# Strassen's seven products for the gate and up projections of a decoder block on one Trainium2 core

## What is computed

```python
h2 = rmsnorm(x, norm2_w[layer]) * (1.0 + sc2) + sh2
ffn = (jax.nn.silu(h2 @ w_ffn_gate[layer]) * (h2 @ w_ffn_up[layer])) @ w_ffn_down[layer]
x = x + g2 * ffn
return rmsnorm(x, final_norm_w)
```

## Time and profile before

| | |
|---|---|
| time, 3 runs | 1796.13 to 1798.64 us, median 1796.4 |
| the profiled execution's own time | 1798.21 us |
| its span, first to last instruction | 1796.4 us |
| TensorE matmul busy | 1673.2 us, 93% |
| VectorE busy | 851.3 us, 47% |
| ScalarE busy | 619.6 us, 34% |
| GpSimd busy | 282.8 us, 16% |
| mean granted TensorE clock | 0.968 |
| DMA over the span | 154.76 MB, mean 86 GB/s |

### The profile page before, as it was taken

One profiled execution on the slowest core, in us unless ns is written; L12 is line 12 of the kernel. 1 busy time (PEld: TensorE's weight loads), 2 busy tenths in 40 slices (PEclk: granted clock), 3 DMA queues, 4 the chain that ended last, 5 costly groups with the idle time before them and its releaser, 6 DMA issues.

```text
span 1796.4 us, 21138 instructions
## 1 busy us (share of the span) xinstructions
PE 1673.2 (93%) x8115; PEld 1355.4 (75%) x8115; DVE 851.3 (47%) x1412; ACT 619.6 (34%) x941; POOL 282.8 (16%) x215
## 2 busy tenths in 40 slices
PE   4997999999999989999999789999999999999996
PEld 2783477888888868877877568888888887887875
DVE  4677999654856667554434631111111111234333
ACT  5326412355665665562123321111111111232232
POOL 1311022244443522230002200000000000002002
PEclk8998999999999999999999889999999999999998
DMA  9561211321212150003443301111111111422231
GB/s 330 186 231 42 71 48 47 100 77 47 65 47 71 59 182 1 1 1 129 153 164 123 111 24 47 52 53 47 47 47 47 47 49 56 188 93 82 101 128 52
DMA packets 124293, 154.76 MB, mean 86 GB/s; under 512 B 8382, under 2 KB 90425, under 8 KB 124220
## 3 DMA queue, kind: packets, MB, share of 16 engines
q1 hardware_dynamic: 115578, 134.91, 22.8%
q10 hardware_dynamic: 8066, 16.78, 2.5%
q0 software_dynamic: 576, 2.10, 0.3%
HBM read 132.25 MB, written 20.99 MB: 85 GB/s over the span
## 4 chain that ended last, share of the span: by engine, by line
PE 73%; issue 14%; DVE 6%; ACT 3%; POOL 2%; DMA 1%; SPq 0%; POOLq 0%; DVEq 0%; ACTq 0%
PE pp L502 20%; PE pp L504 19%; PE pp L503 19%; PE pp L1258 5%; PE pp L1264 3%; PE pp L1443 3%; PE pp L1552 2%; DVE arena L1808 2%; DVE h_tmp L2129 1%; POOL x L822 1%; PE pp L1281 1%; DVE h_raw L1778 0%; ACT arena L975 0%; POOL x1b L827 0%; DVE h_lo L2135 0%
## 5 line engine op out<-in xcount | busy, mean ns | idle before, releaser
L497 DVE TENSOR_TENSOR w_lo<-raw,w_hi 128x1024 fp32r<-128x1024 f32 x112 | 142.5, 1273 | 441.8 <-ACT w_hi L492 441.8
L492 ACT ACTIVATE w_hi<-raw 128x1024 fp32r<-128x1024 f32 x112 | 118.6, 1059 | 523.9 <-PE pp L504 523.9
L502 PE MATMUL pp<-h_hi,w_hi 128*128 128x512 f32 x704 | 276.0, 392 | 13.6 <-DVE h_lo L2135 13.6
L503 PE MATMUL pp<-h_lo,w_hi 128*128 128x512 f32 x704 | 275.6, 391 | 0.0
L504 PE MATMUL pp<-h_hi,w_lo 128*128 128x512 f32 x704 | 275.5, 391 | 0.0
L502 PE MATMUL pp<-hT_hi,e_hi 128*128 128x512 f32 x416 | 168.2, 404 | 7.4 <-POOL hT_lo L721 6.0
L1830 DVE TENSOR_SCALAR_CACHE_REDUCE arena<-arena,bound 128x384 bf16<-128x384 f32 (+2 forms) x192 | 169.4, 941 | 0.8
L502 PEld LDWEIGHTS pp<-h_hi,w_hi 128*128 128x128 f32 x704 | 133.3, 189 | 41.8 <-DVE h_lo L2135 14.1
L504 PE MATMUL pp<-hT_hi,e_lo 128*128 128x512 f32 x416 | 164.3, 395 | 0.0
L503 PE MATMUL pp<-hT_lo,e_hi 128*128 128x512 f32 x416 | 164.2, 395 | 0.0
L503 PEld LDWEIGHTS pp<-h_lo,w_hi 128*128 128x128 f32 x704 | 133.3, 189 | 27.8
(11 more groups left out here) (229 smaller groups left out, 2816.8 us busy)
## 6 DMA issues: line engine op xcount, KB each, us to landing
arena<-in_w_ada SPq DMA_DIRECT2D x48, 512.0 KB, 8.0
raw<-in_w_ffn_down SPq DMA_DIRECT2D x44, 512.0 KB, 3.2
arena<-in_w_in SPq DMA_DIRECT2D x33, 512.0 KB, 3.6
raw<-in_w_ffn_gate SPq DMA_DIRECT2D x22, 512.0 KB, 3.6
raw<-in_w_ffn_up SPq DMA_DIRECT2D x22, 512.0 KB, 3.7
gates_t<-arena ACTq DMA_DIRECT2D x32, 256.0 KB, 2.1
gate_in<-gates_t SPq DMA_DIRECT2D x8, 1024.0 KB, 5.3
raw<-in_w_out SPq DMA_DIRECT2D x16, 512.0 KB, 3.2
```

What stands on the lines that cost most here:

```text
L492: act.activation(w_hi[n % 2][:, :], raw[:, n % 4, :], ACT.Copy).then_inc(hi_ready, 1)
L497: dve.tensor_tensor(w_lo[n % 2][:, :], raw[:, n % 4, :], w_hi[n % 2][:, :].bitcast(F32), ALU.subtract).then_inc(lo_ready, 1)
L502: nc.tensor.matmul(out, ah, bh, start=start and k == 0, stop=False)
L503: nc.tensor.matmul(out, ah, bl, start=False, stop=False)
```

## The change

Two hidden tiles form a pair (11 pairs). For each pair and each matrix (m = 0 gate, m = 1 up) the product is a 2x2 block product: two hidden tiles by two feature halves, times two feature halves by two token halves. Strassen's scheme does it in seven block products instead of eight. A block product is four k slices of 128x128 by 128x512, 12 matmuls. The order of the 14 products of a pair is in `FIRST` and `LATER`; every engine's queue is written as steps n, in which it first does what follows from product n-4 and then prepares the weights of product n.

- The sums of weight blocks are new: GpSimd (`weight_sum`) for five of seven products, then ScalarE (hi) and VectorE (lo), 512 wide, in a ring of four buffers.
- The sums of h2 blocks (`cb_sum`) are made once, during the first pair, by GpSimd and VectorE; all seven combinations are kept as hi and lo.
- The results of products 2, 5 and 1 are copied out of their banks by ScalarE, mixed by GpSimd (`mix_parts`), and VectorE adds the other products' banks (`combine`, six steps for each matrix and pair).
- ScalarE's Silu and VectorE's product with it (`gate_hidden`) follow once for each of four blocks. The hidden values go to memory (`hid_d`, two stores of 512 KB for each pair, issued by SP) and come back for the down steps, 256 KB a step, in the same queue as the weights.
- The hardware loop now has four passes over two pairs (28 products); three pairs stand ahead of it.

The diff, cut to its core (GpSimd's and ScalarE's side of the h2 combinations, buffer addresses and the renaming of one helper are left out):

```diff
-    h2_hi, h2_lo = rounded("h2_hi", 24576, KD, SEQ), rounded("h2_lo", 32768, KD, SEQ)
-    xn2 = [x1[:, t, :] for t in range(4)] + [own(f"xn2_{t}", B0 + D * t, D) for t in range(4)]
-    h2_tmp = [own(f"h2_tmp{i}", D0 + HALF * i, HALF) for i in range(2)]
-    hidT = own("hidT", A0, KF * SEQ)
+    COMBO = {2: 24576, 4: 28672, 1: 0, 3: 4096, 5: 8192, 7: 12288, 6: 16384}
+    cb_hi = {q: rounded(f"cb_hi{q}", o, 4, HALF) for q, o in COMBO.items()}
+    cb_lo = {q: rounded(f"cb_lo{q}", o + 2048, 4, HALF) for q, o in COMBO.items()}
+    cb_sum = {q: own(f"cb_sum{q}", o + 2048, 4, HALF) for q, o in COMBO.items()}
+    h2_part = [[own(f"h2_part{f}{t}", 32768 + 2048 * (f + 2 * t), 4, HALF) for t in range(2)] for f in range(2)]
+    xn2 = [x1[:, t, :] for t in range(4)] + [own(f"xn2_{t}", B0 + D * t, D) for t in range(4, NT)]
+    wp_at = [22528, 23552, 40960, 41984]
+    wp_hi = [rounded(f"wp_hi{i}", o, HALF) for i, o in enumerate(wp_at)]
+    wp_lo = [rounded(f"wp_lo{i}", o + HALF, HALF) for i, o in enumerate(wp_at)]
+    wp_sum = [own(f"wp_sum{i}", o + HALF, HALF) for i, o in enumerate(wp_at)]
+    stage = [own(f"stage{j}", 36864 + SEQ * j, SEQ) for j in range(2)]
+    hid_in = [own(f"hid_in{i}", 34816 + HALF * i, HALF) for i in range(4)]
...
+    FF_PAIRS = KF // 2
+    FIRST = [(m, q) for q in (2, 4, 5, 1, 3, 7, 6) for m in range(2)]
+    LATER = [(m, q) for m in range(2) for q in (2, 5, 1, 4, 3, 7, 6)]
+    PER = len(FIRST)
+    S_DN = S_FF + PER * FF_PAIRS
+    PEELED, TURNS = 3, (FF_PAIRS - 3) // 2
+    WEIGHTS_OF = {1: ((0, 0), (1, 1), ALU.add), 2: ((1, 0), (1, 1), ALU.add), 3: ((0, 0),), 4: ((1, 1),), 5: ((0, 0), (0, 1), ALU.add),
+                  6: ((1, 0), (0, 0), ALU.subtract), 7: ((0, 1), (1, 1), ALU.subtract)}
+    INPUTS_OF = {1: ((0, 0), (1, 1), ALU.add), 2: ((0, 0),), 3: ((0, 1), (1, 1), ALU.subtract), 4: ((1, 0), (0, 0), ALU.subtract), 5: ((1, 1),),
+                 6: ((0, 0), (0, 1), ALU.add), 7: ((1, 0), (1, 1), ALU.add)}
+    BANK_OF = {2: 0, 5: 1, 1: 2, 4: 3, 3: 0, 7: 1, 6: 2}
+    COMBO_ORDER = [2, 4, 5, 1, 3, 7, 6]
+    COPIED = (2, 5, 1)
+    COPY_BEFORE = {3: 2, 7: 5, 6: 1}
+    STEPS_OF = {4: (0,), 3: (1,), 7: (2, 3), 6: (4, 5)}
+
+    def product(n):
+
+        p, x = divmod(n, PER)
+        m, q = (LATER if p else FIRST)[x]
+        return p, x, m, q
...
+    def steps_at(p, m, q):
+
+        if p == 0 and m:
+            return {7: (0, 1, 2, 3), 6: (4, 5)}.get(q, ())
+        return STEPS_OF.get(q, ())
...
+        def ffn_tile(p, m, i=0):
 
             for j in range(2):
-                for m, w in enumerate((wg, wu)):
-                    n = S_FF + 2 * j + m
-                    sp.wait_ge(lo_ready, i * 4 + (n - 3))
-                    sp.dma_start(raw[:, n % 4, :].rearrange("p (k c) -> p k c", c=P), w[:, :, bass.ds(i * 256 + j * P, P)]).then_inc(raw_full[n % 4], 16)
-
-        ffn_tiles(0)
-        with sp.Fori(1, KF // 2) as i:
-            ffn_tiles(i)
+                sp.dma_start(raw[:, 2 * m + j, :].rearrange("p (k c) -> p k c", c=P),
+                             (wg, wu)[m][:, :, bass.ds(i * 512 + (p * 256 + j * P), P)]).then_inc(raw_full[2 * m + j], 16)
+
+        def store_hidden(p, i=0):
+
+            sp.wait_ge(hid_ready, i * 8 + (4 * p + 4))
+            for j in range(2):
+                sp.dma_start(hid_d[bass.ds(i * 512 + (p * 256 + j * P), P), :], stage[j]).then_inc(hid_stored, 16)
...
+        def pair_tiles(p, i=0):
+
+            for m in range(2):
+                sp.wait_ge(lo_ready, i * (2 * PER) + (S_FF + (PER * (p - 1) + 7 * (m + 1) if p > 1 else 13 + m)))
+                ffn_tile(p, m, i)
+            store_hidden(p - 1, i)
...
+                u = th * KF + f
+                if u < 4 and isinstance(i, int):
+                    sp.wait_ge(lo_ready, S_DN - (7 if u < 2 else 0))
+                else:
+                    sp.wait_ge(st_lo, i * 4 + (ST_DN + u - 3))
+                sp.dma_start(raw[:, u % 4, :].unsqueeze(1), wd[:, bass.ds(i * 4 + f, 1), :]).then_inc(raw_full[u % 4], 16)
+                sp.dma_start(hid_in[u % 4], hid_d[bass.ds(i * 512 + f * P, P), th * HALF:(th + 1) * HALF]).then_inc(raw_full[u % 4], 16)
+
+        down_steps(0, range(4))
+        store_hidden(FF_PAIRS - 1)
+        down_steps(0, range(4, 10))
...
+        def weight_sum(n, i=0):
+
+            p, x, m, q = product(n)
+            if len(WEIGHTS_OF[q]) < 3:
+                return
+            a, b, op = WEIGHTS_OF[q]
+            for r in range(2):
+                pool.wait_ge(raw_full[2 * m + r], ff_raw(p, i))
+            pool.wait_ge(w_used, i * (2 * PER) + (S_FF + n - 3 if n >= 4 else S_FF - 1))
+            pool.tensor_tensor(wp_sum[n % 4], ff_weight(m, a), ff_weight(m, b), op).then_inc(sum_ready, 1)
+
+        def mix_parts(p, m, i=0):
+
+            two, five, one = (part_at[(m, q)] for q in COPIED)
+            pool.wait_ge(part_copied, i * 12 + max(copy_rank(p, m, q) for q in COPIED))
+            if p:
+                pool.wait_ge(hid_stored if m else hid_ready, i * (64 if m else 8) + (32 if m else 4) * p)
+            pool.tensor_tensor(out_part(m, 0), one, five, ALU.subtract).then_inc(mixed, 1)
+            pool.tensor_tensor(out_part(m, 3), one, two, ALU.subtract).then_inc(mixed, 1)
+
+        def product_done(n, i=0):
+
+            p, x, m, q = product(n)
+            if x in ((3, 10) if p else (7, 10)):
+                if n == 10:
+                    pool.wait_ge(h2_sum_dve, 8)
+                mix_parts(p, int(x == 10), i)
...
+        weight_sum(0)
+        weight_sum(1)
+        for k in range(4):
+            combo_sum(4, k)
+        for n in range(4, PEELED * PER):
+            product_done(n - 4)
+            weight_sum(n)
+            if n in (5, 7, 9, 11):
+                for k in range(2):
+                    combo_sum({5: 1, 7: 3, 9: 7, 11: 6}[n], k)
+        with pool.Fori(0, TURNS) as i:
+            for n in range(PEELED * PER, (PEELED + 2) * PER):
+                product_done(n - 4, i)
+                weight_sum(n, i)
+        for n in range(PER * FF_PAIRS - 4, PER * FF_PAIRS):
+            product_done(n)
...
+        def weight_hi(n, i=0):
+
+            p, x, m, q = product(n)
+            of = WEIGHTS_OF[q]
+            if len(of) == 3:
+                act.wait_ge(sum_ready, i * 20 + rank(n, (1, 2, 5, 6, 7)))
+                src = wp_sum[n % 4]
+            else:
+                act.wait_ge(raw_full[2 * m + of[0][0]], ff_raw(p, i))
+                act.wait_ge(w_used, i * (2 * PER) + (S_FF + n - 3 if n >= 4 else S_FF))
+                src = ff_weight(m, of[0])
+            act.activation(wp_hi[n % 4][:, :], src, ACT.Copy).then_inc(hi_ready, 1)
+
+        def silu(p, m_tile, t, i):
+
+            s = 2 * m_tile + t
+            act.wait_ge(combined, i * 24 + combine_rank(p, 0, {2: 0, 1: 1, 0: 3, 3: 5}[s]))
+            act.activation(silu_buf[s], silu_buf[s], ACT.Silu).then_inc(silu_ready, 1)
+
+        def product_done(n, i=0):
+
+            p, x, m, q = product(n)
+            act.wait_ge(w_used, i * (2 * PER) + (S_FF + n + 1))
+            if q in COPIED:
+                act.activation(part_at[(m, q)], bank[4 * m + BANK_OF[q]], ACT.Copy).then_inc(part_copied, 1)
+            if x == (6 if p else 12):
+                silu(p, 1, 0, i)
+                silu(p, 0, 1, i)
+                if p == 0:
+                    silu(p, 0, 0, i)
+            if x == 7 and p:
+                silu(p, 0, 0, i)
+            if x == (8 if p else 13):
+                silu(p, 1, 1, i)
...
+        def strassen(n, i=0):
+
+            p, x, m, q = product(n)
+            pe.wait_ge(lo_ready, i * (2 * PER) + (S_FF + n + 1))
+            if p == 0:
+                pe.wait_ge(h2_ready, 4 * (COMBO_ORDER.index(q) + 1))
+            if q in COPY_BEFORE:
+                pe.wait_ge(part_copied, i * 12 + copy_rank(p, m, COPY_BEFORE[q]))
+            elif p:
+                pe.wait_ge(combined, i * 24 + combine_rank(p - 1, m, 5))
+            split_product(bank[4 * m + BANK_OF[q]], [(wp_hi[n % 4][:, k * P:(k + 1) * P], wp_lo[n % 4][:, k * P:(k + 1) * P],
+                                                      cb_hi[q][:, k, :], cb_lo[q][:, k, :]) for k in range(4)]).then_inc(w_used, 1)
...
+        for n in range(4):
+            strassen(n)
         turn_xn2(1)
-        pe.wait_ge(h2_ready, 2 * KD)
-        for m in range(2):
-            hidden(0, m, 1)
-        for m in range(2):
-            for hf in range(2):
-                hidden(1, m, hf)
-        with pe.Fori(1, KF // 2) as i:
-            for j in range(2):
-                for m in range(2):
-                    for hf in range(2):
-                        hidden(j, m, hf, i)
+        pe.wait_ge(t2_read, 2 * KD)
+        for n in range(4, PEELED * PER):
+            strassen(n)
+        with pe.Fori(0, TURNS) as i:
+            for n in range(PEELED * PER, (PEELED + 2) * PER):
+                strassen(n, i)
...
```

(92 more changed lines are left out.)

213 lines of the change are left out of this document (108 added, 105 removed).

## The result

The changed kernel takes **1752.7 us** (median of 4 runs, 1748.6 to 1753.3), the kernel before beside it 1796.3 (1795.9 to 1798.6): the ratio is 0.9747, with an interval of 0.9735 to 0.9758, 43.6 us less. The forecast was 1751 us with 1742 to 1769. The sum was right; one of its terms was too low, two were too high, and one of its reasons does not hold. That the three misses (+2.4, -1.0 and -0.7 us) nearly cancel is luck.

A forecast was written before the change was run, and what follows sets the result against it. TensorE was taken as the bound, the gate and up loop costing its matmuls times 0.2267 us. Terms -59.8 + 1.0 + 10 + 3.3 = -45.5 us took the profiled 1798.21 to 1752.7, as median 1751 us; range 1742 to 1769.

The forecast's parts named there:

- Fewer matmuls: Gate and up loop: 1848 matmuls instead of 2112, at 0.2267 us each, 59.8 us less.
- No waits in the ten later pairs: Steady loop: the other engines keep up with TensorE's 38.1 us a pair; 0, upper end +30 us.
- Output projection to product 4: From the output projection's end to product 4's start: +1.0 us, bounds -2 and +4.
- The first pair: Products 4 to 14, with VectorE's extra sums and rests: +10 us, bounds 0 and +29.
- The slowdown beside GpSimd: VectorE operations with both inputs in SBUF: +0.28 us each beside GpSimd, 18 of them in a pair.
- Rival 1: First pair: VectorE and GpSimd exclude each other, all 23 us of GpSimd block; +19, 1770 us; chance 0.14.
- Rival 3: Steady loop: GpSimd blocks VectorE in every pair, 45.1 us a pair; slower than before, 1840 us; chance 0.04.
- Rival 2: Loop late once in each pair, at VectorE's queue or the loop's turn; 2 us for ten pairs, 1771 us; chance 0.14.
- The handover: Last gate and up matmul to first down matmul: 6.4 us instead of 3.1, +3.3 us; bounds +1 and +6.
- Memory: Hidden values' stores and loads through memory: 0, upper end +3 us.

The follow-up runs named there:

- e1: Changed kernel with product 6 of each matrix and pair made twice, eight products instead of seven: 1810.6 us, 1.008 of the kernel before.
- e4: Changed kernel with GpSimd making each weight sum twice from the second pair on: 1821.8 us, 1.0137 of the kernel before.
- e12: Changed kernel plus a GpSimd operation that reads and writes SBUF behind each weight sum of ten pairs: 1765.2 us, 0.9828 of the kernel before.
- e5: The changed kernel again, unchanged, timed beside other follow-up kernels: 1752.9 us, 0.9754 of the kernel before.
- e2: Changed kernel with GpSimd's two gate mixes of the first pair cut to 8 of 512 columns: 1751.0 us, 0.9747 of the kernel before.
- e3: Changed kernel with most of the hidden values' stores and loads through memory cut to two rows a tile: 1752.5 us, 0.9756 of the kernel before.
- e6: Changed kernel with GpSimd's last two first-pair combination sums issued earlier and its gate mixes one step later: 1749.0 us, 0.9734 of the kernel before.
- e8: Changed kernel with the first down step prepared on ScalarE and VectorE before the last two products' combine steps: 1743.6 us, 0.9699 of the kernel before.
- e11: Changed kernel plus a GpSimd operation that only writes SBUF behind each weight sum of ten pairs: 1753.6 us, 0.9761 of the kernel before.
- e7: Changed kernel with GpSimd's eight combination sums of the first pair moved to VectorE: 1756.2 us, 0.9768 of the kernel before.
- e10: Changed kernel with GpSimd's first-pair sums earlier, gate and up mixes later, and the first down step prepared earlier: 1745.2 us, 0.9716 of the kernel before.

## Why the prediction was right, and where not

**Fewer matmuls: -59.8, right.** 1848 matmuls, 0.2267 us apart, at granted clock 1.00 from the second pair on. e1 gives the matmuls back and gets 57.7.

**No waits in the ten later pairs: right in this kernel, but with less slack than argued.** VectorE's 21.0 us a pair are near the 20.6 counted without GpSimd, not the 25.6 with it: in after only part of the summed weights' rests are held up by a GpSimd operation (0.88 us on average, 0.69 or 1.10 each in the steady loop), the gated products none (0.684). What was missing in the argument is how close the edge is: e4 adds 15 us of GpSimd time a pair (to 34.6 us in a pair of 44.9) and pays 7.6 in nine of ten pairs, e12 adds 11.5 us and pays 1.4. The slack was argued as 8.2 us against 4.8 or 6.2 in VectorE's queue, as if the queue began on time; in e4 it takes 8.1 us and begins 5.1 us late.

**Output projection to product 4: forecast +1.0, measured 0.0.** Product 0 comes 18.2 us after the output projection instead of 19.4 before; the forecast had it 1.4 later, so it was too late by 2.5. GpSimd's last residual add ends 7.0 us after the output projection, where 8.9 was taken from the earlier trace rows: VectorE has no 1024-wide weight rests to make around its gatings any more. And the nine operations for product 0 take 6.2 us, not 6.8. Product 2 then waited 3.3 us, where none was forecast, since its differences came later than the early products 0 and 1 wanted them. Both are without weight: product 4 starts 45.0 us after the output projection here, in e5 (where that wait is 1.0 us and the half clock fills the rest) and in most other kernels.

**The first pair: forecast +10, measured +12.4**, and +13.0 in e5. From product 4 on 1799 x 0.2267 = 407.8 us are matmuls; 422.97 leaves 15.1, of which 8.9 are waits before products 8, 10, 12 and 14 (4.6, 0.9, 2.8, 0.5) and 6.2 half clock; before had 2.7 of that. The forecast had 10 of waits and 2.9 of half clock. So the waits were slightly less than forecast, and the mis-sized term is the half clock: it was counted once, behind product 4, and came again behind the waits of 4.6 and 2.8 us, where 7 and 8 matmuls are 0.2 us longer each, 3.4 us with the steps between the clocks. The batches of combinations were rightly named as the place. That waits of 8.9 came near 10 is partly luck, since 4 of the 10 rested on the slowdown that the next paragraph corrects. No reordering made the waits less: their sum is 8.9 to 9.5 us in after, e2, e3, e5, e6 and e8 to e12. Why it stays there in e2 and e6, where VectorE is busy for 4 us less, is shown only for its last part, the mix that gets stuck before product 14.

**The slowdown beside GpSimd: the step that failed in kind.** The prediction took +0.28 us for every VectorE operation with two SBUF inputs. VectorE's timeline in the first pair (the four rests from 1059.65), then GpSimd's:

```profile
1059.65 6.81 DVE L2346 TENSOR_TENSOR cb_lo<-cb_sum,cb_hi 128x512 fp32r<-128x512 f32 x4
1066.39 3.46 DVE L2330 TENSOR_TENSOR wp_lo<-wp_sum,wp_hi 128x512 fp32r<-128x512 f32 x2
```

```profile
1059.55 1.34 POOL L934 TENSOR_TENSOR wp_sum<-raw 128x512 f32<-128x512 f32 x1 [8.42 <-PE pp L520]
1060.97 1.62 POOL L942 TENSOR_TENSOR bias<-c_wide,arena 128x512 f32<-128x512 f32 x1
1062.54 1.72 POOL L943 TENSOR_TENSOR bias<-c_wide,arena 128x512 f32<-128x512 f32 x1
1064.22 1.70 POOL L934 TENSOR_TENSOR wp_sum<-raw 128x512 f32<-128x512 f32 x1
1065.88 3.41 POOL L962 TENSOR_TENSOR cb_sum<-h_part,h_part 128x512 f32<-128x512 f32 x2
```

Six VectorE operations take 10.2 us, 1.7 each, and the GpSimd ones beside them 1.6 to 1.7 each: one for one, in turn. The first rest starts at 1059.65, while the sum runs to 1060.89, and ends 0.55 us after it; the mix from 1060.97 ends 1.15 us after that rest. That is no slope of 0.28; it is exclusion. With the rule of the Trainium skill (SBUF — State Buffer, section "Who interferes with whom"), that a VectorE instruction with two SBUF inputs and a GpSimd one that reads SBUF shut each other out, the runs agree: rests at 1.7 us against 0.68 here, and no slowdown beside writes alone (e11)., on which the prediction set it aside, shows the same when taken apart: of its eight operations six took 0.68 or 0.69 us, as they met no GpSimd operation or started ahead of it, and two took 1.77 and 1.78. The mean of 0.96 hid that.

**Rival 1 (+19) did not come, although its mechanism did.** It let all 23 us of GpSimd block VectorE. But combine steps, which read a bank, keep their 0.69 us beside GpSimd's sums, and GpSimd's work often falls where VectorE has none of the other kind: of the 44 VectorE operations from product 4 to 14, 30 keep to 0.7 us or less. e2 takes 4 us off VectorE's busy time there and nothing off the sum of the waits. **Rival 3** is the same mechanism at a higher load, and e4 is what it looks like; there the bound is a late start and how GpSimd's operations meet the queue of gated products, not, as the prediction had it, that both engines' sum exceeds 38.1 us: VectorE was busy for 62 of 100 us there and GpSimd for 75.

**Rival 2** did not come: no gap at the loop's turns, 380.70 us for 380.6 of matmuls. The Trainium skill (Runtime: NRT & Kernel Launch, section "Instruction fetch mechanics") says that a taken branch whose target lies outside the fetched window must wait for a fetch. No run here shows such a cost.

**The handover: forecast +3.3, measured +2.64**, all of it VectorE's queue, as e8 shows. The queue from the first combine step to the hidden rest takes 5.55 us, not 6.0: VectorE's operations were counted at their length of 0.68 to 0.69 us, but in a row they start 0.60 us apart (four in 2.49). What the forecast did not ask is whether the place was worth an edit: with the wait and the half clock behind it, 9.3 us are to be had there.

**Memory: forecast 0, measured 0** (e3).

**The sum** against the trace of before is -59.8 + 0.0 + 12.4 + 2.6 = -44.8, beside -45.5 forecast; the other 4.8 of the profiled 49.6 lie in the two stretches that the change does not touch. Left open are why e6 and e8 do not add up in the medians, what sets how many slow matmuls follow a wait, and what other orders of the first pair would give.

## What to carry to other kernels

When a change takes work from the bounding engine, count the saving from the pitch of its instructions, and look for the give-back at the seams: the first pass, before the rhythm is set, and the handover to the next stage, where one reordered queue was worth as much as the whole first pair's waits. GpSimd time is not free VectorE time: count how many of its operations read SBUF while VectorE has two-input work queued in front of something urgent, and look the other way too, for an urgent GpSimd operation behind a row of VectorE's. A mean over a group can hide operations of 0.68 and 1.78 us; look at the single ones. When a wait is taken away, add up all waits of the place before trusting the gain.

## What was unexpected of the hardware

- A VectorE operation with two SBUF inputs (512 columns, float32) takes 0.68 us alone and advances once per 1.7 us beside back-to-back GpSimd operations that read SBUF. Beside a 0.95 us GpSimd operation that only writes, it stays at 0.69. The other way round, a GpSimd mix behind a row of such VectorE operations took 3.49 us instead of 1.3 (e2, e7; 3.48 in e6).
- In after, the waits of 3.3, 4.6 and 2.8 us before products 2, 8 and 12 were followed by 6, 7 and 8 matmuls of 0.63 us (0.43 apart instead of 0.227, granted clock 0.50); those of 0.9 and 0.5 us by none. So a wait of 3 us cost near to 5 there. It need not: 2.5 us before product 8 and 2.8 before product 14 in e2, and 3.0 before product 14 in e10, were followed by none.
- The same kernel's untouched first part ended between 1003.3 and 1007.2 us in thirteen traces, so single traces can't settle 3 us.
